# The first tile's gate logits moved beside the second tile's norms and attention, weights held behind the last gathers, and six picks held back per feed

## The chip, the cores and the metric

One core of a Trainium2 chip runs the kernel. The time is that of the device, in microseconds, the median of several executions; lower is better.

## The reference

256 tokens of width 1024 (two tiles of 128) go through two blocks in f32. The first has two layers: a mixer and a feed-forward by experts each.

```
for i in range(2):
    h = rms_norm(x, attn_norm[i])
    x = x + (even_mixer if i == 0 else mla_mixer)(h, ...)     # causal attentions
    h = rms_norm(x, ffn_norm[i])
    x = x + peer_ffn(h, peer_w_q[i], peer_sub_keys[i], peer_u[i], peer_v[i])
x = rms_norm(x, final_norm)
```

`peer_ffn` routes each token, by top-16 choices among product keys of 8 heads, to 128 experts: rows of two tables of 16384 x 1024 per layer. An expert's dot product with the token goes through gelu and is weighted by a share, and the row of the other table is added with that weight. The second block then does

```
h = rms_norm_2(x, mix_norm_g)
ys, gate_logit = _token_mixers(h, w_in, ...)       # four attentions: stick-breaking, dilated, forgetting, differential
branch = einsum('bsnc,ncd->bsnd', ys, w_branch)    # 4 branches of 256 -> 1024
gates = sigmoid(gate_logit)                        # h @ the last 4096 columns of w_in
x = x + sum(gates * branch, axis=2) @ w_out
h = rms_norm_2(x, mlp_norm_g)
x = x + square(relu(h @ w_up)) @ w_down
```

## The kernel before, in words

**Stages.** The program is a list of stages; each has a part for TensorE (PE), ScalarE (ACT) and VectorE (DVE), and all three wait for each other at a stage's end. SP streams the weights through a ring of four slots (`wring`, 1 MB each, 128 x 2048 f32), in the order in which `weights()` was called; block n is sent when slot n - 4 is given back. A semaphore says for each block when that is: when TensorE has used it (`given_back`), or, where weights are split, when both halves are made.

**Two kinds of product.** Most projections are plain f32 matmuls. The profile shows each as two records. In the second block's last stages weights and activations are split into two fp32r parts, high by a cast on ScalarE (`split_act`, L486) and low by a subtraction on VectorE (`split_dve`, L493), and a product is three matmuls (`product`, L499 to L501), one record each.

**Experts.** For each tile and layer a feed of 128 picks is opened. A pick is one indirect DMA on POOL's queue (L2092) that fetches, for each of the 128 tokens, one row of 2048 f32: 1 MB. The rows land in a ring of eight places. Then VectorE forms the dot (L1264), ScalarE gelu, weight and a 128x128 diagonal (L1280, L1281, L1289), and TensorE adds diagonal x rows in four records (L1300); some picks are added by VectorE instead (L1272). Each of these is done in the order of picks, each engine lagging the one ahead by one pick. The picks of a feed are given out at points inside the stages of the other tile's work (`point`, `handed_out`): at most 0.6 per unit of weight, and such that all 128 are given out at the end of the work beside them. `finish_experts` does the rest and adds the sums to x (L1360). The order of work is: layer 0's mixer and routing of tile 0; tile 1's beside the picks of tile 0; layer 1's mixer and routing of tile 0 beside the picks of tile 1, and so on; the last feed runs beside the second block's norms, projection (`project_first`), attention (`attend_second(0, ...)`) and norm of differences of tile 0. POOL makes the masks of the second block at pick 388, the fourth of the last feed, once the stages up to tile 1's routing are done, drains, and goes on with its gathers.

**Attention.** `attend` works through groups of up to four heads. TensorE makes the scores (L657) of a group into one of the banks of `maps_in`, VectorE scales, masks and finds the maximum (L768 to L780), ScalarE exponentiates (L731, L727), TensorE turns the probabilities (L666), ScalarE copies them out (L704), TensorE sums the values (L680). With two banks (`two_scores`) the scores are made one group ahead; the second bank is the one that picks are summed in, so attentions beside picks have one bank (`scores`) and there the scores of a group are made when its turn comes. Each group has two points for picks.

**After the last pick.** Tile 1 is normed twice (L333 to L352), turned and split (L520 to L535; `whole` is the unsplit copy), and `project_last` makes its 4612 columns by ten blocks of 8 plain matmuls (L1689). Then comes `attend_second(1, two_scores, ...)` with eight groups: forgetting, stick-breaking, four joint (dilated), two of differences. Then the **gate stage**: for each of 4 branches and 2 halves of 512 columns, gate products of both tiles (2 x 8 x 3 matmuls) and branch products of both tiles (2 x 2 x 3), a sigmoid (L1940), and multiplication and addition on VectorE (L1954 to L1958). `w_out`, norm, `w_up`, `w_down` and the last norm follow.

## Time and profile before

| | us |
|---|---|
| median of three runs | 2356.85 |
| lowest, highest | 2355.56, 2357.27 |
| the profiled execution | 2355.4 |
| its span, first to last instruction | 2353.6 |
| TensorE busy | 1757.5 (75%) |
| VectorE busy | 1455.8 (62%) |
| ScalarE busy | 799.3 (34%) |
| POOL busy | 634.9 (27%) |

DMA moves 744.79 MB, of which the gathers are 536.90. Times inside the span are counted from its start. A row of a timeline has start, duration, engine, line, operation, output and inputs, shape and count, and in brackets how long the engine was idle before it and what released it. PEld is TensorE's load of the stationary operand. The share of DMA is that of the core's 16 DMA engines; a granted clock of 1.00 is 2.4 GHz, 0.50 is 1.2 GHz.

### The profile page before, as it was taken

Reading aid. Unit: us, or ns where it says so; the run is one execution under the profiler, and the core shown is the slowest. Engines: PE = TensorE matmul, PEld = TensorE weight load, DVE = VectorE, ACT = ScalarE, POOL = GpSimd, SP = SyncE. Lnnn points to the kernel's source line nnn. Section 1 sums busy time; section 2 is a strip of 40 time slices with the busy share of each in tenths; the row PEclk is TensorE's granted clock in tenths of the full one; section 3 lists DMA queues with packets and bytes.
Section 4 is the critical chain, followed back from the end, with each engine's and each line's share of the span. In section 5 each row is a group of like instructions: output and inputs, shape, how many; then the busy total and the mean of one; then the engine's idle time right before and its main releaser. Section 6 shows DMA issues by size and latency. Waiting matters only on the chain.

```text
span 2353.6 us, 20971 instructions
## 1 busy us (share of the span) xinstructions
PE 1757.5 (75%) x6686; PEld 1075.5 (46%) x6686; DVE 1455.8 (62%) x2950; ACT 799.3 (34%) x2057; POOL 634.9 (27%) x524
## 2 busy tenths in 40 slices
PE   6587878757777875776786576754885967987987
PEld 3473333523333453232445322743342445866976
DVE  1448754798656479875548986667565145644644
ACT  1211453223325322432442244112664134333532
POOL 0001433444433344443224443434451000000000
PEclk9598999779899988989988898876998966998999
DMA  8068998999999999999979998999995720443442
GB/s 289 20 243 317 417 380 329 420 408 423 381 417 421 367 421 393 394 418 421 382 286 421 369 396 371 420 422 395 359 421 221 283 72 36 182 194 116 177 156 98
DMA packets 106525, 744.79 MB, mean 316 GB/s; under 512 B 12848, under 2 KB 13744, under 8 KB 18352
## 3 DMA queue, kind: packets, MB, share of 16 engines
q0 software_dynamic: 73728, 536.90, 55.9%
q1 hardware_dynamic: 30240, 198.67, 21.9%
q10 hardware_dynamic: 2448, 7.87, 0.9%
q8 instruction: 55, 0.90, 0.2%
q14 instruction: 54, 0.44, 0.0%
HBM read 742.35 MB, written 1.05 MB: 316 GB/s over the span
## 4 chain that ended last, share of the span: by engine, by line
PE 40%; DVE 23%; DMA 21%; ACT 9%; issue 5%; DVEq 1%; POOLq 0%; POOL 0%; PEldq 0%; ACTq 0%; SPq 0%
DMA sb_work<-in_peer_uv,sb_expert 18%; PE ps_acc L1300 11%; DVE sb_work L1264 5%; PE bank L437 4%; PE bank L1130 3%; DVE sb_x L1272 3%; PE bank L499 3%; PE bank L500 2%; PE bank L501 2%; PE bank L680 2%; DMA sb_wring<-in_peer_w_q 2%; ACT sb_probs L731 2%; PE ps_acc L1689 2%; PE ps_acc L501 1%; PE ps_acc L499 1%
## 5 line engine op out<-in xcount | busy, mean ns | idle before, releaser
L1300 PE MATMUL ps_acc<-sb_work,sb_diag 128*128 128x512 f32 x1464 | 746.5, 657 | 284.6 <-ACT sb_diag L1289 223.6
L2092 POOL DMA_INDIRECT sb_work<-in_peer_uv,sb_expert x512 | 632.5, 1235 | 1148.0 <-PE ps_acc L1300 521.6
L1264 DVE CUSTOM_DVE_ANT_0 sb_work<-sb_work,sb_h 128x1024 f32<-128x1024 f32 x512 | 617.3, 1222 | 212.4 <-DMA sb_work<-in_peer_uv,sb_expert 196.3
L1300 PEld LDWEIGHTS ps_acc<-sb_work,sb_diag 128*128 128x128 f32 x1464 | 289.3, 209 | 686.9 <-issue 678.3
L1280 ACT ACTIVATE sb_dots<-sb_dots 128x1 f32<-128x1 f32 x512 | 102.4, 200 | 614.2 <-DVE sb_dots L1264 584.3
L1272 DVE SCALAR_TENSOR_TENSOR sb_x<-sb_work,sb_weight,sb_x 128x1024 f32<-128x1024 f32 x146 | 186.8, 1280 | 51.8 <-ACT sb_weight L1281 51.8
L493 DVE TENSOR_TENSOR sb_work_r<-sb_wring,sb_work_r 128x2048 fp32r<-128x2048 f32 (+1 forms) x60 | 127.1, 2146 | 85.8 <-ACT sb_work_r L486 85.8
L437 PE MATMUL bank<-sb_wring,sb_hT 128*128 128x512 f32 (+2 forms) x392 | 158.4, 563 | 23.3 <-DVEq L278 16.3
L1281 ACT ACTIVATE sb_weight<-sb_dots,sb_share 128x1 f32<-128x1 f32 x512 | 150.8, 294 | 16.6
L1289 ACT ACTIVATE sb_diag<-sb_ident,sb_weight 128x128 f32<-128x128 f32 x366 | 147.0, 402 | 17.6 <-PE ps_acc L1300 5.7
L1130 PE MATMUL bank<-sb_hT,sb_wring 128*128 128x128 f32 x1024 | 125.4, 287 | 22.4 <-DMA sb_wring<-in_peer_w_q 20.0
L1130 PEld LDWEIGHTS bank<-sb_hT,sb_wring 128*128 128x128 f32 x1024 | 123.6, 203 | 26.0 <-issue 24.7
L486 ACT CAST sb_work_r<-sb_wring 128x2048 fp32r<-128x2048 f32 (+1 forms) x60 | 105.6, 1791 | 82.2 <-PE ps_acc L501 44.9
L437 PEld LDWEIGHTS bank<-sb_wring,sb_hT 128*128 128x128 f32 x392 | 73.0, 196 | 108.9 <-issue 103.3
L680 PE MATMUL bank<-sb_work,sb_probsT 128*128 128x64 f32 x336 | 60.4, 346 | 55.2 <-ACT sb_probsT L704 55.2
L500 PE MATMUL bank<-sb_work_r 128*128 128x512 f32 (+1 forms) x256 | 88.7, 346 | 0.0
L680 PEld LDWEIGHTS bank<-sb_work,sb_probsT 128*128 128x128 f32 x336 | 55.4, 254 | 65.8 <-ACT sb_probsT L704 63.2
L1545 PE MATMUL bank<-sb_hT,sb_wring 128*128 128x128 f32 (+1 forms) x448 | 62.7, 310 | 29.4 <-issue 22.4
L501 PE MATMUL bank<-sb_work_r 128*128 128x512 f32 x208 | 83.2, 400 | 0.0
L1545 PEld LDWEIGHTS bank<-sb_hT,sb_wring 128*128 128x128 f32 (+1 forms) x448 | 61.4, 206 | 31.1 <-issue 31.1
L500 PE MATMUL ps_acc<-sb_work_r 128*128 128x256 f32 (+1 forms) x224 | 73.6, 328 | 0.0
L499 PE MATMUL bank<-sb_work_r 128*128 128x512 f32 x128 | 51.7, 404 | 12.8 <-DVE sb_work_r L493 12.8
(287 smaller groups left out, 2114.4 us busy)
## 6 DMA issues: line engine op xcount, KB each, us to landing
sb_wring<-in_w_mix SPq DMA_DIRECT2D x36, 1024.0 KB, 9.0
sb_wring<-in_peer_w_q SPq DMA_DIRECT2D x32, 1024.0 KB, 10.9
sb_wring<-in_hyb_w_in SPq DMA_DIRECT2D x20, 1024.0 KB, 4.9
sb_wring<-in_w_gate SPq DMA_DIRECT2D x16, 1024.0 KB, 4.9
sb_wring<-in_w_up SPq DMA_DIRECT2D x16, 1024.0 KB, 4.8
sb_wring<-in_w_down SPq DMA_DIRECT2D x16, 1024.0 KB, 4.8
sb_wring<-in_mla_w_uq SPq DMA_DIRECT2D x12, 768.0 KB, 10.1
sb_wring<-in_hyb_w_out SPq DMA_DIRECT2D x8, 1024.0 KB, 6.1
```

Of the source, the lines that this page charges most:

```text
L437: last = e.matmul(u.ap[:, 0:bn], xT[:, k0 + k, t * P:(t + 1) * P], sl[:, k, b0:b0 + bn], start=k0 + k == 0, stop=k0 + k == chunks - 1)
L499: pe.matmul(ps, left[0], right[0], start=start, stop=False)
L500: pe.matmul(ps, left[0], right[1], start=False, stop=False)
L501: return pe.matmul(ps, left[1], right[0], start=False, stop=stop)
L680: last = e.matmul(u.ap[:, o * HD:(o + 1) * HD], probsT[:, n % 2, c, i, :], g["values"][i](c), start=first, stop=final)
L1130: last = e.matmul(u.ap[:, j * P:(j + 1) * P], slot_ap(s)[:, k, j * P:(j + 1) * P], hT[:, k0 + k, t * P:(t + 1) * P], start=k0 + k == 0, st ...
L1264: e.tensor_tensor_reduce(u, u, h[:, t, :], 1.0, 0.0, ALU.mult, ALU.add, dots[:, i:i + 1]).then_inc(dot_ready, 1)
L1272: e.scalar_tensor_tensor(x[:, t, :], ring[:, n % RING, D:2 * D], weight[:, k:k + 1], x[:, t, :], ALU.mult, ALU.add).then_inc(slot_free[n % ...
L1281: scaled = e.activation(weight[:, k:k + 1], dots[:, k:k + 1], ACT.Copy, scale=share[:, t, k:k + 1])
L1289: e.activation(diag[:, number % DIAGS, :], ident[:, :], ACT.Copy, scale=weight[:, k:k + 1]).then_inc(diag_ready, 1)
L1300: last = e.matmul(ps_acc[:, b * 512:(b + 1) * 512], diag[:, number % DIAGS, :], ring[:, n % RING, D + b * 512:D + (b + 1) * 512], start=k ...
L2092: pool.indirect_dma_start(ring[:, n % RING, :], None, a["peer_uv"], bass.IndirectOffsetOnAxis(ap=expert[:, t, n % P:n % P + 1], axis=0)).t ...
```

## The change

- `handed_out` gives a feed's picks out up to 122 rather than 128 beside other work, so that six more are left for `finish_experts`.
- In `attend` the scores are made one group ahead with one bank too. With one bank ScalarE empties the turned probabilities before its exponentials, and does the picks of both points after them. Other products can be put into a group (`beside`).
- POOL makes the masks at pick 376 rather than 388, and waits for the stages before tile 1's routing only.
- Gate logits of tile 0 are now made from `hT` by plain f32 products, 8 blocks of 512 columns (`gate_first`), and kept in `first_gates`, which lies in the ring that the gathers have left: two of them in a stage with both norms of tile 1 (`enter_second`, formerly two stages), six in the second to seventh group of its attention.
- SP sends the first weight block of `enter_second`, and all behind it, once the third-last pick has landed (`asides`, `HELD`).
- In the gate stage only tile 1's gate logits are left: plain in the first half of a branch, split in the second. The gate weights are therefore read twice, 16 MB more. The splits of tile 0's activations (in `diff_norm`) go.

```diff
+HELD_BACK = 6
+EARLY_GATES = 2
+HELD = 3
...
-            return f["first"] + int(weight * min((P - f["first"]) / max(f["weight"], 1.0), RATE))
+            return f["first"] + int(weight * min((P - HELD_BACK - f["first"]) / max(f["weight"], 1.0), RATE))
...
-                for g in plan[:ahead]:
-                    score(g)
+                score(plan[0])
                 for n, g in enumerate(plan):
-                    if n and ahead:
+                    if n:
                         turn_probs(n - 1, plan[n - 1])
-                    if n + ahead < len(plan):
-                        score(plan[n + ahead])
+                    if n + 1 < len(plan):
+                        score(plan[n + 1])
                     g["points"][0]("pe", e)
-                    if n and not ahead:
-                        turn_probs(n - 1, plan[n - 1])
+                    if apart[n]:
+                        apart[n]["pe"](e)
                     if n:
                         sum_values(n - 1, plan[n - 1])
...
-                    g["points"][0]("act", e)
+                    if n and one_bank:
+                        empty_turns(e, n - 1, plan[n - 1])
+                    if not one_bank:
+                        g["points"][0]("act", e)
...
-                    if n:
+                    if n and apart[n - 1]:
+                        apart[n - 1]["act"](e)
+                    if n and not one_bank:
                         empty_turns(e, n - 1, plan[n - 1])
+                    if one_bank:
+                        g["points"][0]("act", e)
                     g["points"][1]("act", e)
...
+        def gate_first(b):
+
+            slots = [(weights(gate_block(k, b * 512), 4, 512), k) for k in (0, 4)]
+            u = products.take()
+            given_back[slots[0][0]] = w_used.sem, w_used.plan()
+            given_back[slots[1][0]] = u.full_at()
+
+            def pe(e):
+                u.wait_free(e)
+                for s, k0 in slots:
+                    slot_wait(e, s)
+                    for k in range(4):
+                        last = e.matmul(u.ap, hT[:, k0 + k, 0:P], slot_ap(s)[:, k, :], start=k0 + k == 0,
+                                        stop=k0 + k == DC - 1)
...
+            def act(e):
+                u.wait_full(e)
+                e.copy(first_gates[:, b * 512:(b + 1) * 512], u.ap).then_inc(u.free, 1)
...
+        def enter_second():
+
+            parts = [norm_parts(X, dst, D, g, [1]) for dst, g in ((X, a["final_norm"]), (H, a["mix_norm_g_2"]))]
+            apart = [gate_first(b) for b in range(EARLY_GATES)]
...
         latent(1)
+        mixed_free = len(stages)
         feed_forward(1, [1])
-        mixed_free = len(stages)
...
-        norm(X, X, D, a["final_norm"], [1])
-        norm(X, H, D, a["mix_norm_g_2"], [1])
+
+        asides[len(stream)] = lambda sp: sp.wait_ge(row_landed[(len(gathers) * P - HELD) % RING],
+                                                    16 * ((len(gathers) * P - HELD) // RING + 1))
+        enter_second()
         turn_split(H, x_pair, [1], whole)
         project_last()
-        attend_second(1, two_scores, last_tmp, last_bias, last_cum)
+        attend_second(1, two_scores, last_tmp, last_bias, last_cum,
+                      lambda n: gate_first(EARLY_GATES + n - 1) if 0 < n <= 8 - EARLY_GATES else None)
...
+            for n, half, slots, ms, mb, ug, ub, _, _ in plan:
+                ug.wait_free(e)
+                for i, s in enumerate(slots):
+                    if half:
+                        split_wait(e, ms[i])
+                        right = halves_of(ms[i])
+                    else:
+                        slot_wait(e, s)
+                    for k in range(4):
+                        first, final = 4 * i + k == 0, 4 * i + k == DC - 1
+                        if half:
+                            last = product(e, ug.ap, chunk_of(x_pair, 4 * i + k, 1), [r[:, k, :] for r in right],
+                                           first, final)
+                        else:
+                            last = e.matmul(ug.ap, whole[:, 4 * i + k, :], slot_ap(s)[:, k, :], start=first, stop=final)
...
-                if n == 3 * P + 4:
+                if n == 2 * P + 120:
```

Lines of the changed kernel are some 7 to 32 higher than those of the kernel before (L657 is now L664, L1300 L1313, L1689 L1686, L2092 L2124; `gate_first`'s matmuls are L1765, the plain ones of the gate stage L1944).

TensorE in layer 1's attention of tile 1, from the first group on, before (L1300 are picks, two matmuls each):

```order
L657 MATMUL ps_scores<-sb_work 128x256 x4
L1300 MATMUL ps_acc<-sb_work,sb_diag 128x512 x10
L657 MATMUL ps_scores<-sb_work 128x256 x4
L1300 MATMUL ps_acc<-sb_work,sb_diag 128x512 x6
L666 MATMUL ps_turn<-sb_ident,sb_probs 128x128 x8
L680 MATMUL bank<-sb_work,sb_probsT 128x64 x8
L1300 MATMUL ps_acc<-sb_work,sb_diag 128x512 x6
```

and in the changed kernel:

```order
L664 MATMUL ps_scores<-sb_work 128x256 x8
L1313 MATMUL ps_acc<-sb_work,sb_diag 128x512 x10
L673 MATMUL ps_turn<-sb_ident,sb_probs 128x128 x8
L664 MATMUL ps_scores<-sb_work 128x256 x4
L1313 MATMUL ps_acc<-sb_work,sb_diag 128x512 x4
L687 MATMUL bank<-sb_work,sb_probsT 128x64 x8
L1313 MATMUL ps_acc<-sb_work,sb_diag 128x512 x6
```

The scores of the second group now stand beside those of the first, and each later group's one group earlier; the turning stands ahead of the first point's picks rather than behind them.

TensorE in the second block's attention of tile 1, from the first group on, before:

```order
L657 MATMUL ps_scores<-sb_work 128x256 x4
L657 MATMUL ps_acc<-sb_work 128x256 x4
L666 MATMUL ps_turn<-sb_ident,sb_probs 128x128 x8
L657 MATMUL ps_scores<-sb_work 128x256 x3
L680 MATMUL bank<-sb_work,sb_probsT 128x64 x8
L666 MATMUL ps_turn<-sb_ident,sb_probs 128x128 x8
L657 MATMUL ps_acc<-sb_work 128x256 x3
L680 MATMUL bank<-sb_work,sb_probsT 128x64 x8
```

and in the changed kernel:

```order
L664 MATMUL ps_scores<-sb_work 128x256 x4
L664 MATMUL ps_acc<-sb_work 128x256 x4
L673 MATMUL ps_turn<-sb_ident,sb_probs 128x128 x8
L664 MATMUL ps_scores<-sb_work 128x256 x3
L1765 MATMUL bank<-sb_wring,sb_hT 128x512 x8
L687 MATMUL bank<-sb_work,sb_probsT 128x64 x8
L673 MATMUL ps_turn<-sb_ident,sb_probs 128x128 x8
L664 MATMUL ps_acc<-sb_work 128x256 x3
L1765 MATMUL bank<-sb_wring,sb_hT 128x512 x8
L687 MATMUL bank<-sb_work,sb_probsT 128x64 x8
```

A gate block of eight matmuls now stands between the next scores and the sums of values, in six groups.

POOL, the gathers on both sides of the masks (`sb_mixed`), before:

```order
L2092 DMA sb_work<-in_peer_uv,sb_expert 128x2048 x388
L2084 IOTA sb_mixed 128x256
L2086 MEMSET sb_mixed 128x256
L2087 AFFINE_SELECT sb_mixed<-sb_mixed 128x256
L2092 DMA sb_work<-in_peer_uv,sb_expert 128x2048 x124
```

and in the changed kernel:

```order
L2124 DMA sb_work<-in_peer_uv,sb_expert 128x2048 x376
L2116 IOTA sb_mixed 128x256
L2118 MEMSET sb_mixed 128x256
L2119 AFFINE_SELECT sb_mixed<-sb_mixed 128x256
L2124 DMA sb_work<-in_peer_uv,sb_expert 128x2048 x136
```

The masks moved from behind the fourth pick of the last feed to eight picks ahead of its first.

## Rows read from the trace of the kernel before

**Rows 1.** Busy time by stretch: length, five engines (instructions), PEclk, DMA share, GB/s.

```profile
214.00:1794.00 1580.00, 1134.44 (x3810) 602.25 (x3811) 1098.90 (x2246) 579.14 (x1732) 633.26 (x515) 0.88 0.97 395
320.00:400.00 80.00, 66.30 (x227) 34.70 (x226) 36.72 (x68) 36.32 (x103) 23.86 (x22) 0.94 0.83 322
585.00:600.00 15.00, 10.59 (x21) 4.14 (x20) 9.61 (x16) 7.41 (x19) 5.86 (x6) 0.89 0.83 323
780.00:820.00 40.00, 36.04 (x106) 17.29 (x105) 15.82 (x33) 14.50 (x45) 14.08 (x12) 0.93 0.90 341
1160.00:1240.00 80.00, 66.66 (x224) 36.72 (x223) 35.56 (x65) 34.41 (x97) 21.66 (x20) 0.91 0.78 295
1400.00:1425.00 25.00, 14.56 (x29) 5.48 (x28) 15.64 (x32) 11.84 (x28) 6.64 (x9) 0.86 0.63 245
1590.00:1630.00 40.00, 13.55 (x80) 12.64 (x80) 32.77 (x43) 8.77 (x31) 22.58 (x15) 0.64 1.01 420
1640.00:1700.00 60.00, 48.44 (x138) 21.80 (x136) 34.22 (x73) 35.41 (x88) 26.62 (x23) 0.91 0.88 343
1700.00:1780.00 80.00, 68.50 (x207) 31.37 (x205) 54.39 (x125) 48.40 (x134) 41.69 (x34) 1.00 1.01 421
1780.00:1800.00 20.00, 14.86 (x32) 6.28 (x33) 12.68 (x28) 10.99 (x30) 1.66 (x2) 0.91 0.67 279
```

**Rows 2.** Timeline, one group of layer 1's attention of tile 1.

```profile
1166.99 5.37 PE L1300 MATMUL ps_acc<-sb_work,sb_diag 128*128 128x512 f32 x12
...
1172.20 1.89 PE L657 MATMUL ps_scores<-sb_work 96*128 96x256 f32 x8
...
1174.22 1.22 DVE L771 SCALAR_TENSOR_TENSOR sb_probs<-ps_scores,sb_causal 128x1024 f32<-128x1024 f32 x1 [9.84 <-PE ps_scores L657]
...
1177.36 1.04 PE L666 MATMUL ps_turn<-sb_ident,sb_probs 128*128 128x128 f32 x8
...
1179.06 1.28 ACT L731 ACT_TABLE_LOAD   x1
...
1183.47 3.65 PE L680 MATMUL bank<-sb_work,sb_probsT 128*128 128x64 f32 x16 [5.08 <-ACT sb_probsT L704]
...
1185.25 0.40 ACT L1289 ACTIVATE sb_diag<-sb_ident,sb_weight 128x128 f32<-128x128 f32 x1
...
1194.46 1.89 PE L657 MATMUL ps_scores<-sb_work 96*128 96x256 f32 x8
```

**Rows 3.** Timeline of POOL at the end of the third route beside picks.

```profile
1404.71 0.93 POOL L2092 DMA_INDIRECT sb_work<-in_peer_uv,sb_expert  x1 [12.63 <-DVE sb_expert L1233]
...
1410.06 0.40 POOL L2087 TENSOR_SCALAR_AFFINE_SELECT sb_mixed<-sb_mixed 128x256 f32<-128x256 f32 x1
1422.59 0.96 POOL L2092 DMA_INDIRECT sb_work<-in_peer_uv,sb_expert  x1 [12.13 <-issue]
```

**Rows 4.** Timeline, from the last pick's sum into the second tile.

```profile
1803.65 1.28 DVE L1360 TENSOR_TENSOR sb_x<-sb_x,ps_acc 128x512 f32<-128x512 f32 x2 [4.51 <-PE ps_acc L1300]
...
1816.14 1.97 PE L520 MATMUL ps_turn<-sb_ident,sb_h 128*128 128x128 f32 x8 [12.53 <-ACTq L278]
...
1832.04 7.03 PE L1689 MATMUL bank<-sb_wring,sb_probsT 128*128 128x512 f32 x16
```

**Rows 5.** Busy time by stretch: second tile's attention, two joint groups, gate stage.

```profile
1894.00:1966.00 72.00, 49.93 (x200) 41.05 (x200) 40.12 (x93) 25.19 (x55) 0.00 (x0) 0.55 0.04 15
1931.30:1945.10 13.80, 13.80 (x50) 11.08 (x49) 7.04 (x20) 3.90 (x8) 0.00 (x0) 0.50 0.00 1
1977.50:2094.00 116.50, 111.33 (x480) 91.64 (x480) 62.40 (x51) 47.59 (x41) 0.00 (x0) 0.96 0.46 177
```

**Rows 6.** Groups by line, 1977 to 2141, mean ns of one; then the page's DMA issues.

```profile
L493 DVE TENSOR_TENSOR sb_work_r<-sb_wring,sb_work_r 128x2048 fp32r<-128x2048 f32 x20 | 45.4, 2285 | 4.3 <-ACT sb_work_r L486 4.3
...
L486 ACT CAST sb_work_r<-sb_wring 128x2048 fp32r<-128x2048 f32 x20 | 37.7, 1904 | 2.6 <-DVEq L278 1.7 <-DMA sb_wring<-in_w_gate 0.9
...
sb_wring<-in_w_gate SPq DMA_DIRECT2D x16, 1024.0 KB, 4.9
```

More of the change, by code:

```diff
@@ L476, in halves_of @@
             n = chunks * (c1 - c0)
-            return [places[place][:, i * SLOT:i * SLOT + n].rearrange("p (c n) -> p c n", c=chunks)
-                    for i in range(2)]
+            half = places[place].shape[1] // 2
+            return [places[place][:, i * half:i * half + n].rearrange("p (c n) -> p c n", c=chunks) for i in range(2)]
         def split_act(e, m):
@@ L619, in dve_stage, with attend @@
             stage(dve=dve, points=points)
-        def attend(groups, maps_in=scores):
+        def attend(groups, maps_in=scores, beside=lambda n: None):
             plan = []
-            ahead = len(maps_in.views) - 1
+            apart = []
+            one_bank = len(maps_in.views) == 1
             for g in groups:
@@ L631, in attend @@
                 chunks = g["tile"] + 1
-                value = {"s": maps_in.take(), "turns": [turns.take() for _ in range(chunks)], "out": products.take(),
+                apart.append(beside(len(plan)))
+                if plan:
+                    plan[-1]["out"] = products.take()
+                value = {"s": maps_in.take(), "turns": [turns.take() for _ in range(chunks)],
                          "n_out": n_out, "n_turned": n_turned, "chunks": chunks, "w": P * chunks,
@@ L640, in attend @@
                 plan.append(g | value | {"points": [point(6.0), point(6.0)]})
+            plan[-1]["out"] = products.take()
             def sums_of(n):
@@ L1886, in build @@
                     branch = weights(w_branch[n].rearrange("(p n) -> p n", p=P), 2, D)
-                at = 3 * len(plan)
-                ms = [plan_split(s, 4, 0, 512, (at + i) % 4) for i, s in enumerate(slots)]
-                ms.append(plan_split(branch, 2, half * 512, half * 512 + 512, (at + 2) % 4))
-                ug = [products.take() for _ in range(TILES)]
+                ug = products.take()
                 ub = [spare_banks.take() for _ in range(TILES)]
-                split_back[ms[0]] = w_used.sem, w_used.plan()
```

170 lines of the change are left out of this document (74 added, 96 removed).

## The prediction

> **What bounds the kernel now.** I first read the busy time in stretches over the whole span. While experts are gathered (214 to 1794 us) the DMA engines are busy 0.97 of the time and move 395 GB/s, with no compute engine near its limit; where they are full the row reads 1.01 and 421 GB/s, which is one pick of 1.05 MB in 2.5 us [rows 1]. So this stretch is bound by bytes, and what can be won in it is bytes taken out, or time in which DMA is not full. The same rows show where that time is: the attentions with one bank of scores (shares 0.83, 0.90, 0.78 and 0.88), the ends of the three routes that run beside picks (0.83 over 15 us at the first, the second much like it, and 0.63 over 25 us at the third), and the last 20 us. After 1794 nothing is gathered: DMA is at 0.04 in the second tile's attention and 0.46 in the gate stage, and TensorE sets the pace, in the first at a granted clock of 0.55, in the second at 0.96 with 111 of 116.5 us busy [rows 5]. Next I read the order of instructions in time, for one attention group, for POOL's queue at the third route's end, and for the passage out of the gathers.
>
> **The change, part by part.** Gains are negative, in us.
>
> *1. One score bank, next scores ahead.* Before, VectorE waits 9.84 us for each group's scores, because TensorE issues them only after all picks of the group before; from one group's scores to the next it is 22.3 us (1172.20 to 1194.46) [rows 2]. Now the scores stand ready when the group begins, and the chain of a group is: turn the last probabilities (1.04), then what now lies between the table load at 1179.06 and the value sums at 1183.47, table load, four exponentials and the copy of the turned ones (4.4), then table load, weight and diagonal of a pick (to 1185.65, 2.2) [rows 2]: 7.6, less 0.5 as the copy starts on the first half, so 7.1 us, in which TensorE also does the next scores (1.89) and one pick. Then two picks of the first point, the value sums 2.0, three picks of the second, at 1.79 each (5.37 for three) [rows 2]: 7.1 + 3.6 + 2.0 + 5.4 = 18.1 for six picks, 16.3 for five. Before it is 20.4 twice in layer 0's attention, and 20.5 and 22.3 in layer 1's. Against it stands that ScalarE now empties the turned probabilities ahead of the exponentials, so it waits for TensorE's picks; that is in the 7.1. The ends: nothing is gained (the chain is as long), or all DMA idle time in these attentions, 14 + 4 + 18 + 8 = 44 us (each share's distance from 1.01 times its length). I take three cycles each 2.2 shorter in layer 0 (-7), -3 and -8 in layer 1's two, where the picks are five or six, and -3 in the second block's: **-21**. In 1700 to 1780 DMA is full, so nothing is won there.
>
> *2. Six picks held back.* Each feed gives out picks up to 122 rather than 128 beside other work. At a route's end POOL sits 12.63 us until the next experts are there [rows 3] and DMA runs dry for (1.01 - 0.83) x 15 = 2.7 us. With six more picks still to be worked off, the ring is still being filled then, and the gap closes. Two such ends give -5. At the third, POOL also makes the masks, and after them it sends its next gather only 12.13 us later, though the mask's last instruction takes 0.40: its drain ends only after the four gathers in flight have landed [rows 3]. Both together cost (1.01 - 0.63) x 25 = 9.5. Now the masks come eight picks ahead of the new tile's first, where six or more gathers are in flight. The drain waits for those as well, so its 6.7 stays and only the 2.8 of the route goes. **-8** in all; ends 0 and -14.
>
> *3. Weights held.* The two big and two small w_mix blocks that SP fetched ahead in 1590 to 1630, with DMA at 1.01, now go after the gathers: 2.1 MB, 5 us of full DMA: **-5**, ends 0 and -5. What was hidden by them has to be fetched later: four gate blocks are issued when the third-last pick lands. The last two picks are then not alone. In the last 20 us before, DMA is at 0.67, so the last pick lands near 1793.4, and VectorE adds the sums at 1803.65 [rows 1, 4]: 10 us, since the stage of the norm of the differences lies between. With ten dots left for the last stage that shrinks to dot, weight, diagonal and one pick, some 5 us: -5, given back by up to 5 us of shared bandwidth. I take **-2**. The Trainium skill (DMA: Bandwidth & Descriptors, Queues, rings and completion order) says each DMA engine takes turns between the queue rows that have work; by that alone SP's blocks halve the last picks' rate and this term is 0.
>
> *4. Entering the second tile.* Before, 12.5 us pass from the add to the transposes, with TensorE idle 12.53 us [rows 4]. Now two gate products lie there, 7.03 us each at the full clock [rows 4]. Four blocks issued some 5 us before the last pick lands are there 12 us after it (6 MB at 2.5 us, and 2 us to start; a block takes 4.9 us from issue to landing when alone [rows 6]), so the second product ends some 3 us after the norms would have. **+3**, ends 0 and +10.
>
> *5. Six gate products in the second tile's attention.* Joint groups now take 6.9 us each, two in 13.8, TensorE busy throughout at clock 0.50 [rows 5]. One product more doubles the work: at the full clock the group is 3.5 + 7.0 = 10.5, so +3.6 for each of five; the sixth costs nothing, as it falls into the stick group, where the chain is on ScalarE and VectorE (TensorE is idle for 22 of the 72 us, none of them in joint groups). +18, less 4 for what else runs at 2.4 GHz instead of 1.2: **+14**. The ends are +8 (better overlap) and +64 (clock stays at 0.50: 13.7 more for each of five, less 4). I take the first kind, because in 1700 to 1780 TensorE has the same mix of small products and 128x512 picks and shows 1.00 [rows 1]. The Trainium skill (TensorE: Matmul & The Clock Gate, What's actually happening) says that the clock is throttled by default and that activity releases it; taken by busy time, that would put the joint groups at 1.00 already, and the row at 0.50 with 13.8 of 13.8 us busy does not agree, which keeps the fourth rival alive.
>
> *6. Gate stage.* Before, each of the 8 rounds is 60 products of 512 columns: 480 in 111.3 us, of which the first twelve cost 2.4 more at the low clock, so 0.227 each and 13.6 a round [rows 5]. Now an even round has one plain f32 gate product (6.84 for 8 chunks) and 12 products for the branch (2.72): 9.56; an odd one 24 + 12: 8.16. A pair is 17.7 instead of 27.2. Then VectorE: 2 x 2.29 + 2 x 1.22 for splits and 5.5 for gating, 12.5 a pair. DMA: 5 MB, 12.6. The slots: an odd round's second block is issued when the even round's first is used (3.4), lands 4.9 later, is cast in 1.90 and subtracted in 2.29 [rows 6]: 12.5, needed at 12.3. So 17.95. Four pairs are 71.8 against 108.9, and the first round needs no split of its gate weights (4.6): **-41**, ends -30 and -44.
>
> The sum: -21 - 8 - 5 - 2 + 3 + 14 - 41 = **-60**. The profiled run took 2355.4 us (span 2353.6); the median of the three is 2356.85, 1.4 above. The forecast is 2355.4 - 60 = 2295, and as a median 2297.
>
> **Rivals.**
> *Gathers barely faster.* Terms 1 to 3 give 12 instead of 36, since the group's chain waits for TensorE's own picks, or the drain stands in a worse place. For it: ScalarE's new order; against: the wait of 9.84 for scores goes for certain. 2297 + 24 = 2321.
> *Gate stage bound by its slots.* Four slots filled in order must hold five blocks a pair; if a branch block comes late, its split stands at the head of ScalarE's and VectorE's queues, and a pair is 22, not 18: +16, 2313. For it: the 0.2 us of slack missing above; against: DMA is needed for 12.6 of 18.
> *All DMA idle time is won in term 1.* 2297 - 23 = 2274. Against it: TensorE has 16 us of work in a group of six.
> *Clock stays low in the attention.* +50, 2347. For it: the row at 0.50 [rows 5]; against: 7 us pieces of full-width products.
> *Slower.* The clock stays at 0.50 in the attention and in the gate stage too, whose 70.9 us become 142: 2297 + 50 + 71 = 2418. It decides once 10 of the stage's 71 us are lost to it beside the 50. Against it: 0.96 there now, with the same products [rows 5].
> That the change does less than it says is the first rival.
>
> **How the numbers follow.** Forecast 0.60, gathers 0.16, slots 0.10, clock in the attention 0.07, all idle time 0.03, slower 0.04. The forecast's own span is 2280 to 2314. The range of 8 in 10 leaves out the two clock cases (0.11) and some of the edges: 2274 to 2330. A measurement can tell 0.2%, 4.7 us, from no change. Faster by more: 0.60 + 0.16 + 0.10 + 0.03 and 0.05 of the clock case = 0.94; within it 0.02; slower 0.04.
>
> **What would show it.** Right: a DMA share above 0.90 in the layer-1 attention, VectorE's wait for scores gone; no dip at the first two routes' ends; one drain of some 18 us eight picks before the last tile, with some 7 us of idle DMA; the second tile's attention near 86 us long (72 before) at a clock over 0.9; the gate stage near 74 us. Wrong: groups still 20 us apart, a clock of 0.5 in the attention, or rounds of the gate stage that begin with a wait for a split.

## The result, and the profile after

The changed kernel takes 2327.44 us (median of 4 runs, 2324.4 to 2339.23) beside 2356.2 for the kernel before in the same session: ratio 0.988, 95% interval 0.986 to 0.990. It is 28.8 us faster where 60 were forecast, and nearer to the first rival's 2321 than to 2297. It lies inside the range of 2274 to 2330 only because that range was drawn wide enough for the rival; the forecast's own span, 2280 to 2314, missed it.

The trace splits the time cleanly at one instruction, the add of the last picks' sums at the end of the gathers. First VectorE's timeline there, then TensorE's behind it, of the kernel after:

```profile
1800.26 1.29 DVE L1373 TENSOR_TENSOR sb_x<-sb_x,ps_acc 128x512 f32<-128x512 f32 x2 [3.51 <-PE ps_acc L1313]
```

```profile
1801.70 13.97 PE L1765 MATMUL bank<-sb_wring,sb_hT 128*128 128x512 f32 x32 [1.48 <-DVEq L280]
1816.39 0.88 PE L521 MATMUL ps_turn<-sb_ident,sb_h 128*128 128x128 f32 x6 [0.71 <-ACTq L280]
```

Before, this add stood at 1803.65 [rows 4]. Up to it the change gained 3.4 us; from it to the end of the span it took 549.9 before and 526.2 after, a gain of 23.7. The prediction had 36 in front of the add (terms 1 to 3) and 24 behind it (terms 4 to 6: +3, +14, -41). The second half comes out right within a microsecond, partly by luck (terms 5 and 6 miss by some 4 each, in opposite directions, as shown below), so the whole miss lies in the first.

Busy time by stretch of the kernel after, one call of that view: length, five engines (instructions), granted TensorE clock, DMA share, GB/s.

```profile
318.00:321.50 3.50, 0.06 (x1) 0.00 (x0) 2.12 (x4) 3.41 (x11) 1.36 (x1) 0.99 1.00 421
321.50:325.00 3.50, 3.44 (x5) 1.52 (x6) 1.23 (x2) 2.67 (x11) 0.00 (x0) 0.52 1.02 431
1380.00:1400.00 20.00, 9.30 (x20) 3.56 (x21) 12.28 (x20) 7.58 (x19) 8.48 (x8) 0.92 0.63 250
1400.00:1425.00 25.00, 19.90 (x36) 7.55 (x36) 15.07 (x28) 9.69 (x27) 8.73 (x10) 0.86 1.01 423
1786.00:1800.30 14.30, 13.97 (x32) 6.00 (x32) 7.24 (x13) 6.26 (x21) 1.85 (x1) 1.00 1.02 422
...
1988.80:2066.90 78.10, 75.31 (x256) 48.52 (x256) 45.59 (x44) 32.66 (x33) 0.00 (x0) 0.97 0.67 254
585.00:600.00 15.00, 12.09 (x26) 4.16 (x25) 7.37 (x13) 5.39 (x18) 7.46 (x8) 1.00 1.01 421
```

The last row answers to the first route's end: 0.83 before [rows 1], 1.01 now, as forecast; the second route's end, 985 to 1000, reads 1.01 too, where it was 0.80. The third and fourth rows are the third route's end: the dip that stood in 1400 to 1425 (0.63) [rows 1] is gone, and one of the same depth now stands in 1380 to 1400, where the masks are made. POOL's timeline shows the drain behind them:

```profile
1372.98 0.40 POOL L2119 TENSOR_SCALAR_AFFINE_SELECT sb_mixed<-sb_mixed 128x256 f32<-128x256 f32 x1
1389.38 0.96 POOL L2124 DMA_INDIRECT sb_work<-in_peer_uv,sb_expert  x1 [16.01 <-issue]
```

The drain, a wait of POOL for what it has begun (the DMA share is 0.00 in 1386 to 1389, just ahead of the next gather), holds POOL 16.01 us and costs (1.01 - 0.63) x 20 = 7.6 us of DMA, forecast 18 and 7. The fifth row is the last stage of the gathers: eight picks in 13.97 of 14.30 us at the full clock, so TensorE is hardly ever free. The sixth is the gate stage.

The second tile's attention, and in the second fence a stretch of its joint groups, the same view of the kernel after:

```profile
1894.50:1977.30 82.80, 73.78 (x296) 43.75 (x296) 39.54 (x92) 28.32 (x61) 0.00 (x0) 0.94 0.45 164
```

```profile
1931.00:1952.50 21.50, 21.50 (x87) 12.62 (x87) 7.49 (x22) 4.95 (x10) 0.00 (x0) 1.00 0.53 194
```

The clock, 0.50 in these groups before [rows 5], is 1.00 now.

**Where the first half went.** This is the group in layer 0's attention, TensorE's timeline after:

```profile
314.05 1.04 PE L673 MATMUL ps_turn<-sb_ident,sb_probs 128*128 128x128 f32 x8
315.01 1.13 PE L664 MATMUL ps_scores<-sb_work 64*128 64x256 f32 x8
316.08 1.98 PE L1313 MATMUL ps_acc<-sb_work,sb_diag 128*128 128x512 f32 x4
321.56 5.31 PE L1313 MATMUL ps_acc<-sb_work,sb_diag 128*128 128x512 f32 x8 [3.50 <-ACT sb_diag L1302]
326.71 1.89 PE L687 MATMUL bank<-sb_work,sb_probsT 128*128 128x64 f32 x16
328.44 5.37 PE L1313 MATMUL ps_acc<-sb_work,sb_diag 128*128 128x512 f32 x12
333.65 0.60 PE L673 MATMUL ps_turn<-sb_ident,sb_probs 128*128 128x128 f32 x4
```

Four records are one pick. From turning to turning it is 19.60 us, forecast 18.1. The chain to the second pick is 7.51 (forecast 7.1) and the last three picks 5.37 (forecast 5.4), but the two picks between take 5.31, where the prediction had 3.6. TensorE was idle for 3.50 us ahead of them, since ScalarE does a table load, four exponentials and another table load before it can make the next diagonal. In the 3.5 us after that the granted clock is 0.52, nearly all at the lower of its two levels, 1.2 GHz (the first two rows of the table above). The Trainium skill (TensorE: Matmul & The Clock Gate, HAM oscillation — how this bites in real kernels) describes a kernel in which waits for data between bursts of matmuls throttle the engine anew each time; the trace agrees, with 0.52 behind the wait, though here TensorE waits for ScalarE and not for data from DMA. The kernel before pays in the same way, which the prediction did not use. In a group of layer 0's attention it has a hole of 2.61 us ahead of the value sums, and the three picks behind them take 6.87 us and not 5.37, at a granted clock of 0.78 (331.8 to 338.7):

```profile
331.86 6.87 PE L1300 MATMUL ps_acc<-sb_work,sb_diag 128*128 128x512 f32 x12
```

The experiments ask what the hole costs, and what each part of the change gives.

### The profile page after: what moved, and what is told of

It reads as the page before. It is cut to its first block, busy times and chain, and to the rows that moved or that the text cites. A ratio compares the mean times of both kernels' runs of the same rounds, so it can differ in the third digit from the quotient of the medians.

```text
span 2326.5 us, 20848 instructions
## 1 busy us (share of the span) xinstructions
PE 1780.1 (77%) x6626; PEld 1047.3 (45%) x6626; DVE 1429.7 (61%) x2931; ACT 786.7 (34%) x2063; POOL 625.0 (27%) x524
## 3 DMA queue, kind: packets, MB, share of 16 engines
HBM read 759.12 MB, written 1.05 MB: 327 GB/s over the span
## 4 chain that ended last, share of the span: by engine, by line
PE 40%; DVE 21%; DMA 20%; ACT 10%; issue 6%; DVEq 1%; POOLq 1%; PEldq 1%; POOL 0%; ACTq 0%; PEld 0%; SPq 0%
DMA sb_work<-in_peer_uv,sb_expert 17%; PE ps_acc L1313 13%; PE bank L439 4%; DVE sb_work L1277 4%; PE bank L1143 3%; DVE sb_x L1285 3%; PE bank L1765 2%; DMA sb_wring<-in_peer_w_q 2%; PE bank L500 2%; PE bank L687 2%; PE ps_acc L1686 2%; ACT L1293 1%; PE bank L502 1%; PE bank L501 1%; ACT sb_probs L740 1%
## 5 line engine op out<-in xcount | busy, mean ns | idle before, releaser
L1313 PE MATMUL ps_acc<-sb_work,sb_diag 128*128 128x512 f32 x1500 | 774.3, 664 | 295.7 <-ACT sb_diag L1302 253.3
L2124 POOL DMA_INDIRECT sb_work<-in_peer_uv,sb_expert x512 | 622.6, 1216 | 1162.1 <-PE ps_acc L1313 587.9
L1313 PEld LDWEIGHTS ps_acc<-sb_work,sb_diag 128*128 128x128 f32 x1500 | 299.7, 211 | 717.8 <-issue 701.0
L1285 DVE SCALAR_TENSOR_TENSOR sb_x<-sb_work,sb_weight,sb_x 128x1024 f32<-128x1024 f32 x137 | 175.5, 1281 | 51.3 <-ACT sb_weight L1294 51.3
L494 DVE TENSOR_TENSOR sb_work_r<-sb_wring,sb_work_r 128x2048 fp32r<-128x2048 f32 (+1 forms) x52 | 109.9, 2126 | 115.2 <-ACT sb_work_r L487 115.2
L1294 ACT ACTIVATE sb_weight<-sb_dots,sb_share 128x1 f32<-128x1 f32 x512 | 150.8, 294 | 16.6
L487 ACT CAST sb_work_r<-sb_wring 128x2048 fp32r<-128x2048 f32 (+1 forms) x52 | 91.2, 1772 | 120.2 <-PE ps_acc L502 45.0
L1558 PE MATMUL bank<-sb_hT,sb_wring 128*128 128x128 f32 (+1 forms) x448 | 60.0, 303 | 28.8 <-issue 15.7
L710 ACT COPY sb_probsT<-ps_turn 128x512 f32<-128x512 f32 (+2 forms) x48 | 23.9, 532 | 126.3 <-PE ps_turn L673 118.3
L501 PE MATMUL bank<-sb_work_r 128*128 128x256 f32 (+1 forms) x192 | 62.9, 327 | 0.0
L1765 PE MATMUL bank<-sb_wring,sb_hT 128*128 128x512 f32 x128 | 59.0, 617 | 1.5 <-DVEq L280 1.5
L439 PE MATMUL bank<-sb_wring,sb_work 128*128 128x512 f32 x128 | 57.8, 611 | 1.9 <-DVEq L280 1.1
L687 PEld LDWEIGHTS bank<-sb_work,sb_probsT 128*128 128x128 f32 x336 | 45.1, 205 | 20.7 <-issue 10.5
```

Source lines behind the costliest of these rows:

```text
L439: last = e.matmul(u.ap[:, 0:bn], xT[:, k0 + k, t * P:(t + 1) * P], sl[:, k, b0:b0 + bn], start=k0 + k == 0, stop=k0 + k == chunks - 1)
L494: e.tensor_tensor(low, slot_ap(s)[:, :, c0:c1], high, ALU.subtract).then_inc(lo_made.sem, 1)
L501: pe.matmul(ps, left[0], right[1], start=False, stop=False)
L1285: e.scalar_tensor_tensor(x[:, t, :], ring[:, n % RING, D:2 * D], weight[:, k:k + 1], x[:, t, :], ALU.mult, ALU.add).then_inc(slot_free[n % ...
L1294: scaled = e.activation(weight[:, k:k + 1], dots[:, k:k + 1], ACT.Copy, scale=share[:, t, k:k + 1])
L1313: last = e.matmul(ps_acc[:, b * 512:(b + 1) * 512], diag[:, number % DIAGS, :], ring[:, n % RING, D + b * 512:D + (b + 1) * 512], start=k ...
```

## The experiments

Each was timed beside the kernel before, whose median was 2356.2 to 2359.4 in all sessions; against 2357.3 the change's ratio of 0.988 (0.9879) makes 2328.8, and differences to the change are taken from that. Differences of under some 6 us between two kernels are within the intervals. Of the code only the lines that matter are shown; `...` stands for lines left out. Unless said otherwise, the edit is to the changed kernel.

**No picks held back.**

```
-HELD_BACK = 6
+HELD_BACK = 0
```

> The change, but no picks held back: every feed gives out its 128 beside other work again. By term 2 of the prediction the route ends run dry again, 2.7 to 2.8 us each and three of them, and this is 8 us slower than the change (2335), and the last stage has four dots again instead of ten. Rival: six fewer picks given out before a route ends are also 5 in 100 fewer at every point of every attention, where TensorE's and ScalarE's chain sets the length of a group and not DMA, so what is won at a route's end is lost before it; then this is within 3 us of the change (2324 to 2330), and the dip in DMA's share before the attentions of layer 1 (0.92 and 0.85 in 740 to 780 us, where it was 1.01 in the kernel before) is gone.

Measured: 2335.94, ratio 0.991 (0.990 to 0.993). It is 7.1 us slower than the change, little more than the intervals allow, and near term 2's 8. The rival falls: what is won at the routes' ends is not lost ahead of them. In this kernel's trace the dip at the first route's end is back: the DMA share is 0.64 in 590 to 600 us, 1.01 in the change. The last stage has changed as well: from the last gather's issue to the add of the sums it is 19.3 us, 14.1 in the change.

**The old order of a group.** Scores behind the turned probabilities of the group before, and the copy behind the exponentials, with one bank only.

```
-                    if n:
+                    if n and not one_bank:
                         turn_probs(n - 1, plan[n - 1])
-                    if n + 1 < len(plan):
+                    if one_bank:
+                        score(g)
+                    elif n + 1 < len(plan):
                         score(plan[n + 1])
                     g["points"][0]("pe", e)
+                    if n and one_bank:
+                        turn_probs(n - 1, plan[n - 1])
...
```

> The change, but with one bank of scores the old order of an attention group: scores behind the first picks, the turned probabilities copied behind the exponentials. By term 1 of the prediction this is 21 us slower than the change (2348). Rival, from the trace after: a group now lasts 19.6 to 20.4 us instead of 20.4 with six picks, so the order gives 1 to 3 us in each attention and no more; then it is 3 to 8 us slower (2330 to 2336).

Measured: 2328.86, ratio 0.988 (0.986 to 0.990), the change's own. **Term 1 is zero** within the intervals, and the 3 to 8 us expected from the cycles do not show either. TensorE's timeline of this kernel, the same group:

```profile
318.73 1.04 PE L673 MATMUL ps_turn<-sb_ident,sb_probs 128*128 128x128 f32 x8
322.38 3.65 PE L687 MATMUL bank<-sb_work,sb_probsT 128*128 128x64 f32 x16 [2.61 <-ACT sb_probsT L715]
325.81 7.04 PE L1313 MATMUL ps_acc<-sb_work,sb_diag 128*128 128x512 f32 x12
332.79 1.13 PE L664 MATMUL ps_scores<-sb_work 64*128 64x256 f32 x8
```

The old order has a hole of its own, ahead of the value sums, and it costs in the same way: sums 3.65 instead of 1.89, three picks 7.04 instead of 5.37. The new order takes away VectorE's wait for scores (79.5 us in all at one line before, 6.1 now) and puts a hole of 3.50 in place of one of 2.61. Busy time of the four one-bank attentions, each from its first score product to its last value sum, first of the old order, then of the new one (the change):

```profile
292.60:377.50 84.90, 67.16 (x225) 35.52 (x226) 40.64 (x70) 43.73 (x123) 24.89 (x24) 0.90 0.85 336
731.90:797.30 65.40, 52.14 (x161) 26.76 (x162) 31.50 (x62) 36.62 (x107) 26.92 (x21) 0.90 0.94 369
1129.90:1215.50 85.60, 65.89 (x209) 38.19 (x210) 35.59 (x62) 40.26 (x111) 21.74 (x21) 0.84 0.76 288
1634.50:1770.40 135.90, 114.51 (x329) 52.51 (x330) 84.35 (x193) 81.70 (x216) 62.54 (x51) 0.92 0.95 387
```

```profile
294.60:377.50 82.90, 67.42 (x225) 35.07 (x226) 41.42 (x70) 43.02 (x123) 25.83 (x24) 0.86 0.89 341
730.70:800.20 69.50, 53.41 (x161) 27.15 (x162) 32.30 (x62) 36.21 (x107) 22.64 (x21) 0.85 0.91 347
1132.70:1209.10 76.40, 61.48 (x209) 34.61 (x210) 36.27 (x62) 39.87 (x111) 22.46 (x21) 0.89 0.86 322
1629.30:1769.80 140.50, 115.57 (x329) 54.50 (x330) 85.82 (x192) 78.62 (x215) 55.44 (x51) 0.90 0.96 377
sum 369.30, PE 297.88 PEld 151.33 DVE 195.81 ACT 197.72 POOL 126.37; mean PE 74.47 PEld 37.83 DVE 48.95 ACT 49.43 POOL 31.59
```

The new order gains 2.0 and 9.2 in the first and third and loses 4.1 in the second and 4.6 in the fourth: 369.3 against 371.8. The fourth shows where a loss can come from. In 1700 to 1780 us DMA is full in the old order (share 1.01, 421 GB/s, clock 0.96) and no longer in the new one (0.99, 396 GB/s, clock 0.91).

**No hold on SP.** The wait for the third-last pick is taken out.

```
-        asides[len(stream)] = lambda sp: sp.wait_ge(row_landed[(len(gathers) * P - HELD) % RING],
-                                                    16 * ((len(gathers) * P - HELD) // RING + 1))
```

> The change, but SP does not wait for the third-last pick: weights of what follows are fetched as slots come free. By term 3 the last gathers lose 5 us of DMA to them and the tail wins back up to 5: 0 to 7 us slower than the change (2327 to 2334), 5 by the value taken. Rival: in the last 150 us of the gathers DMA is not the bound (387 GB/s at a share of 0.98 in 1720 to 1780, against 421), so bytes taken out of it give nothing, and weights there earlier give the second tile's first products a start: 0 to 4 us faster.

Measured: 2339.36, ratio 0.993 (0.991 to 0.994): 10.6 us slower, more than either theory. A count of bytes accounts for it: SP's queue (packets, MB, share) between 1445 and 1785 us, without the hold, then with it:

```profile
q1 hardware_dynamic: 2880, 20.97, 14.8%
```

```profile
q1 hardware_dynamic: 2304, 16.78, 11.8%
```

4.19 MB, not 2.1, is what the hold keeps out of the gathers, since the two gate products of the entry bring four blocks that SP fetches ahead. At 2.5 us for 1.05 MB that is 10.0 us. That the two agree so closely is luck in part: the profiled execution of this kernel is 6.1 us slower than that of the change (2334.36 against 2328.23), all of it in front of the add, which stands at 1806.66.

**Value sums ahead of the first picks**, with one bank.

```
                         score(plan[n + 1])
+                    if n and one_bank:
+                        sum_values(n - 1, plan[n - 1])
                     g["points"][0]("pe", e)
...
-                    if n:
+                    if n and not one_bank:
                         sum_values(n - 1, plan[n - 1])
```

> The change, but with one bank the value sums of the group before come right behind the next scores, ahead of the first point's picks. In the trace after TensorE stands idle for 3.50 us between the first pick of a group and the second (318.06 to 321.56 us), since ScalarE does table load, four exponentials and table load first, and the granted clock then is 0.52 for 3.5 us, so the two next picks take 5.31 us instead of 3.6. Theory: the value sums (1.9) fill more than half of the hole, the cycle falls from 19.6 to 16.5 to 17.7, and if the cycles of the one-bank attentions bound the gathers there, some 14 cycles give 10 to 25 us: 2302 to 2317. Rival: the picks per group are what bounds, by DMA's 2.5 us each (six are 15) and by dots that come late, and it gives under 5 us.

Measured: **2298.65**, ratio 0.975 (0.974 to 0.977), 30 us faster than the change and a little more than the theory gave. TensorE's timeline:

```profile
313.64 1.04 PE L673 MATMUL ps_turn<-sb_ident,sb_probs 128*128 128x128 f32 x8
314.61 1.14 PE L664 MATMUL ps_scores<-sb_work 64*128 64x256 f32 x8
315.67 2.00 PE L687 MATMUL bank<-sb_work,sb_probsT 128*128 128x64 f32 x16
317.51 1.94 PE L1315 MATMUL ps_acc<-sb_work,sb_diag 128*128 128x512 f32 x4
321.16 8.82 PE L1315 MATMUL ps_acc<-sb_work,sb_diag 128*128 128x512 f32 x20 [1.72 <-ACT sb_diag L1304]
329.82 1.04 PE L673 MATMUL ps_turn<-sb_ident,sb_probs 128*128 128x128 f32 x8
```

16.18 us for the same six picks: the sums have gone into the hole, 1.72 us of it are left, and the five picks behind it take 8.82, all at the full pace. The row below, of this kernel's four attentions together, is 36.4 us under the change's 369.30:

```profile
sum 332.90, PE 276.65 PEld 143.67 DVE 195.62 ACT 198.96 POOL 126.79; mean PE 69.16 PEld 35.92 DVE 48.90 ACT 49.74 POOL 31.70
```

So the gathers there are bound by the group's chain, as the prediction said; the change had made it hardly shorter in sum.

**The gate part alone**: no picks held back, old order, no hold, masks at pick 388.

> The gate part of the change alone: no picks held back, the old order with one bank, the masks at the fourth-last tile's old place (pick 388), no hold on SP. The gathers are then those of the kernel before. By terms 4 to 6 of the prediction this is 24 us faster than before (2333 beside 2357). From the runs so far (held back 7, hold 10.6, order 0 against the change at 2328.8) it would be 2346 if these add up, and then the gate part gives 11. Between them: above 2340 the hold pays for something that the gate part costs, below 2336 the parts of the gather stretch lean on each other.

Measured: 2339.62, ratio 0.993 (0.991 to 0.994), a gain of 17.6. Here the last add is at 1811.91, so what follows it takes 526.8 us, 23.1 less than before: terms 4 to 6 again, without any of the others. In front of it 8.3 us are lost, of which 5 are SP's bytes (20.97 MB in 1445 to 1785 beside 18.89 before); the other 3.3 were not traced. The four parts of the gather stretch then give 10.8 together, while taken out one by one they give 7.1, 0.1, 10.6 and 0.7 (the masks, below), 18.5 in all. The 7.7 between the two would mean that some parts lean on each other. But the change's own time, with an interval of some 5 us to either side, enters this difference three times, so it is not shown. The 2339.62 itself lies between the two cases of the expectation.

**The masks at pick 388 again.**

```
+        feed_forward(1, [1])
         mixed_free = len(stages)
-        feed_forward(1, [1])
...
-                if n == 2 * P + 120:
+                if n == 3 * P + 4:
```

> The change, but the masks are made at pick 388 again, 12 later than in the change. The trace after shows a drain of 15.2 us on POOL at pick 376 and DMA's share at 0.63 in 1380 to 1400 us, where the kernel before had 1.01, and 1.01 in 1400 to 1440, where it had 0.74 and 0.80. By term 2 the dip is the drain's own and is only moved: 0 to 3 us slower than the change (2329 to 2332). Rival: a drain while six or more gathers are in flight costs more than one behind the route's end: then this is 2 to 5 us faster.

Measured: 2329.46, ratio 0.988 (0.987 to 0.990): no difference that can be told. The drain costs about the same at either place.

**No gate products in the attention.** This kernel leaves out six of the eight blocks of the first tile's gate logits, with their weights; it only prices them.

```
-lambda n: gate_first(EARLY_GATES + n - 1) if 0 < n <= 8 - EARLY_GATES else None
+lambda n: None
```

> The change without the six gate products in the second tile's attention (and without their weights and copies), so six of the eight blocks of the first tile's gates are not computed. By term 5 this is 14 us faster than the change in the attention (2315). The rival of a low clock had it at 64. The trace after shows joint groups 10.5 to 10.95 us apart at a granted clock near 1, against 6.9 before at 0.50: 11 us in all, so 2318; if the clock falls to 0.50 again, each group is 6.9 and the two agree.

Measured: 2318.52, ratio 0.983 (0.982 to 0.985): the six products cost 10 us, forecast 14. Without them the clock in the joint groups is 0.50 again (1922 to 1957 us), as in the kernel before, and the attention is 71.4 us long instead of 82.8.

**Value sums first, and none held back in the fourth feed.**

```
+HELD_BACK = (6, 6, 6, 0)
```

> The kernel with the value sums ahead of the first picks (2298.65), and picks held back in the first three feeds alone, none in the fourth: the last stage of the gathers then has four dots and six fewer picks. In the trace after that stage is bound by TensorE's 1.75 us a pick and four gate blocks share its last bytes. If held-back picks cost in the last stage what they save elsewhere, this is 0 to 3 us slower or faster than 2298.65. If the seven that no held-back picks cost were all from the last tail, where DMA ran at 0.67, it is 5 to 8 slower (2304 to 2307). If they were from the three route ends, 0 to 5 faster.

Measured: 2296.74, ratio 0.974 (0.973 to 0.976). No difference that can be told, and the two traces show why. Without held-back picks in the last feed the last gather is issued 4.0 us earlier (1749.4 against 1753.4), and the stretch from there to the add is 4.2 longer (19.5 against 15.3). So in this order they are worth nothing in the last feed, and the 7 us of the first experiment should come from the route ends; with the change's own order that was not run.

**The hole filled, order kept.** Each group's score products three times over, the same values into the same bank.

```
-for i, (q, k) in enumerate(g["maps"]):
+for i, (q, k) in enumerate(g["maps"] * (3 if one_bank and g is not plan[0] else 1)):
...
```

> The change in its own order, but with one bank TensorE issues each group's score products three times over into the same bank (the same values), 2.3 us more work per group, ahead of the first pick; the computation is otherwise whole. This lies in TensorE's hole of 3.50 us. If the hole costs by the granted clock that it leaves (0.52 for 3.5 us, in which the next picks take 5.31 us instead of 3.6), the products keep the clock up, the cycle falls from 19.6 to 17.9, and over some 16 groups of six picks the kernel is 10 to 25 us faster than the change (2304 to 2319), with more work done. If the hole costs by its place alone (the picks cannot begin before ScalarE's second table load), nothing changes, or it is 0 to 10 us slower: 2327 to 2339.

Measured: 2313.76, ratio 0.981 (0.980 to 0.983): **with more work, 14 to 17 us faster than the change** (14 by the two medians, 17 by what each gains on the kernel before in its own session). TensorE's timeline:

```profile
310.98 1.04 PE L673 MATMUL ps_turn<-sb_ident,sb_probs 128*128 128x128 f32 x8
311.95 2.86 PE L664 MATMUL ps_scores<-sb_work 64*128 64x256 f32 x24
314.74 1.98 PE L1313 MATMUL ps_acc<-sb_work,sb_diag 128*128 128x512 f32 x4
318.50 3.67 PE L1313 MATMUL ps_acc<-sb_work,sb_diag 128*128 128x512 f32 x8 [1.78 <-ACT sb_diag L1302]
322.01 1.89 PE L687 MATMUL bank<-sb_work,sb_probsT 128*128 128x64 f32 x16
323.74 5.37 PE L1313 MATMUL ps_acc<-sb_work,sb_diag 128*128 128x512 f32 x12
328.95 1.04 PE L673 MATMUL ps_turn<-sb_ident,sb_probs 128*128 128x128 f32 x8
```

The cycle is 17.97 us, the prediction's 18.1, and the two picks behind the hole take 3.67, its 3.6. The chain to the second pick has not moved (7.52 us, 7.51 in the change); what differs is the granted clock, 1.00 in 318.5 to 322.2. The four attentions are 350.1 us long together, against 369.3, and DMA is full again in 1700 to 1780 (1.01, 421 GB/s). The rival, that the place of the hole alone costs, falls.

**Value sums first, twelve picks held back** (six in the fourth feed).

> The kernel with the value sums ahead of the first picks, and twelve picks held back in the first three feeds, six in the fourth (2298.65 with six in all four, 2296.7 with none in the fourth). If each pick that an attention need not take shortens it where DMA is not the bound, and the ends of the routes have idle DMA for them, it is 3 to 8 us faster (2291 to 2296). If the last stages of a feed are then bound by TensorE's 1.79 us a pick and ScalarE, with DMA full anyway, it is 0 to 8 slower.

Measured: 2309.34, ratio 0.978 (0.976 to 0.980): 7 to 11 us slower than with six (by the ratios and by the medians). Why was not looked into.

**Value sums first, scores twice.**

> The kernel with the value sums ahead of the first picks (2298.65), with each group's score products issued twice into the same bank (1.13 us more for eight of them). There the hole between the first pick and the second is still 1.72 us (319.44 to 321.16). If the clock is still lost in some of its groups (granted 0.91 in the first of the four attentions, 0.95 in the third and fourth), this is 2 to 8 us faster; if what is left is bound by the picks and by ScalarE's chain, the added work falls into the hole and nothing changes (2296 to 2301).

Measured: 2295.93, ratio 0.974 (0.972 to 0.976), no difference that can be told from 2298.65 (0.974 to 0.977).

**The old order, its hole filled.** Each group's transposes twice.

> The change with the old order of an attention group (2328.86), and with one bank each group's transposes of the probabilities issued twice into the same bank (1.04 us more for eight of them); the computation is otherwise whole. In the old order TensorE's hole of 2.61 us lies behind those transposes (319.77 to 322.38), and the three picks behind the value sums then take 7.04 us instead of 5.37. If the clock is what the hole costs in either order, the cycle loses some 1.7 us or more here as well, and it is 8 to 20 us faster than the old order (2309 to 2321), near the change with the filled hole (2313.8): then the new order by itself is worth nothing even at the full clock. If the new order is worth something once the clock holds, this stays at 2322 to 2329, or it is slower by the added work (2329 to 2338).

Measured: 2327.56, ratio 0.987 (0.985 to 0.990), as without them. The theory's number is missed. But the trace shows that the edit did not do what it was for: the hole shrank from 2.61 us to 1.74, and the clock is low behind it nonetheless.

```profile
322.00:326.00 4.00, 3.02 (x17) 2.71 (x18) 0.57 (x2) 3.84 (x10) 0.00 (x0) 0.79 1.02 426
326.00:330.00 4.00, 4.00 (x9) 1.68 (x8) 0.00 (x0) 1.58 (x7) 0.94 (x1) 0.79 0.24 100
```

So what the new order would be worth beside an old one at the full clock stays open. That a hole of 1.7 us spares the clock in one order and not in the other is seen, not explained; in the old order one of 1.38 us ends 3.7 us before it begins. The length of the hole does not settle it in the change either: in its third attention a hole of 3.03 us, up to 1159.54, is followed by a clock of 1.00, and the next one, of 3.04 us up to 1175.78, by 0.55.

## Why the prediction was right and wrong

- **Term 1 (-21): wrong, 0.** The failing step is the sum of the cycle, "7.1 + 3.6 + 2.0 + 5.4 = 18.1", and in it the 3.6 for the two picks of the first point, at 1.79 each. That price holds at the full clock; the chain of 7.1 that stands in the same sum leaves TensorE idle, for 3.5 us as measured, and the picks behind that are granted 0.52 and take 5.31. The cycle is 19.6. With the clock kept up by filler it is 17.97, and 14 to 17 of the 21 us come back. The warning stood in the rows: the value sums of [rows 2], behind a hole of 5.08 us, take 3.65 us where the sum has 2.0 for them, and the granted clock there, 1183.5 to 1187, is 0.50. The prediction weighed the clock for the second tile's attention, by a rival and a page, and not for the groups beside the gathers. It also put the fourth attention's later part, where DMA was full, at no gain and did not ask what could be lost there. Beside the old order the second and fourth attention got longer (+4.1 and +4.6); which of their cycles lose was not taken apart. Its sign of a DMA share above 0.90 in layer 1's attention came for one tile (0.91) and not for the other (0.86).
- **Term 2 (-8): right.** 7 to 8 by its own run; the dips of the first two route ends are gone, and the drain's 7.6 us only moved. The masks' new place is worth nothing that can be told.
- **Term 3 (-5, tail -2): the mechanism right, the account short.** Against the kernel before, 18.89 MB have become 16.78, its 2.1 MB. What it left out is that entering the tile with two gate products would have added 2.1 MB more, so the hold is worth 10.6, of which 5 only undo a cost of the change itself. The tail, from the last gather's issue to the add, got shorter, 20.8 before and 14.1 after, more than the 2 of the forecast. The held-back picks do that, not the hold (14.4 without the hold, 19.3 without held-back picks). But the last gather is issued 3.3 later (1786.2 against 1782.9), where terms 1 to 3 wanted it 34 earlier.
- **What is missing in front of the add.** Of the 33 us 21 are term 1's. Some 5 are the bytes of the two gate products, which no term had. The rest has no cause shown: 3.3 more are lost in front of the add with the gate part alone, and 7.7 lie between the parts together and one by one, which is within the intervals.
- **Term 4 (+3): right.** From the add to the first transposes 16.1 us, 12.5 before: +3.6, with the two products 13.97 long.
- **Term 5 (+14): the mechanism right, the size 10.** The clock was granted as forecast, 1.00, and the joint group is 10.5 us.
- **Term 6 (-41): right within 4.** The stage's gate products begin at 1988.8 and its result is turned from 2066.9, 78.1 us, where a stage near 74 was forecast. With 23.7 gained in all and +3.6 and +10, it gave 37. ScalarE's casts waited 25.0 us in all for branch blocks, the second rival's mechanism, but its 16 us did not happen.
- **The rivals.** "Gathers barely faster", at 0.16, is what happened. Its price was 24 too little gained; 33 was missing. It named the chain that waits for TensorE's own picks, or a badly placed drain, as the cause; the drain is ruled out by its run, and the lower clock behind the hole was in neither. That the result lies near its 2321 is therefore luck in part. The two rivals of a low clock looked for it behind the gathers, where it was 0.94 and 0.97.

## What to carry to other kernels

When a chain of waits is summed for a new order, look also at the clock that TensorE is granted behind each of its waits, in rows of the same kernel. Here a pick priced at 1.79 us took 2.65 behind a hole of 3.5 us, though not every hole cost that. Then the cheapest thing to move is what can fill that hole: here moving the value sums up by a few lines gave as much again as the whole change (2298.65, ratio 0.975, faster than both kernels). And a part that only holds something back should be costed against the change without it, since it may be paying for another part.

## What was not expected of the hardware

- Adding 1.7 us of products to each group, in time that was idle, made the kernel 14 to 17 us faster; in the group taken apart only the granted clock differs, 1.00 instead of 0.52 behind the hole.
- Two holes of the same length in the change's third attention, 3.03 and 3.04 us, left a clock of 1.00 and of 0.55.
- In TensorE's joint groups, busy in every microsecond, the clock is 0.50 with the small products alone [rows 5], and 1.00 with a 7 us piece of 128x512 products between them.
- POOL sends nothing for 16.0 us behind the masks at pick 376 and for 16.6 at pick 388, beside 12.13 before [rows 3]; making them earlier bought nothing that can be told.
